# Top-k selection in a streaming encoder step: two jobs' rounds interleaved, the samples' rounds moved ahead of the delta stage

## The reference, cut to what matters

```python
score = einsum('bqh,bqhk->bqk', iw, relu(dots))           # index scores of every key
score = where(arange(L) < limit, score, -inf)
_, idx = lax.top_k(score, n_top)                            # n_top = min(256, L // 4)
logits = einsum('bqgrd,bqkgd->bqgrk', q, k_all[idx]) * A_HEAD_DIM ** -0.5
p = softmax(where(valid, logits + bias, -inf))
...                                                         # gated delta rule, chunks of 64:
sol = triangular_solve(eye + m, concat([v * beta, kb * exp(gc)]))
```

## Time and profile before

| | us |
|---|---|
| median of 3 runs | 1452.32 (1452.25 to 1454.1) |
| the profiled execution | 1452.18 |
| its span | 1450.3 |
| PE busy | 1395.6 |
| DVE busy | 901.2 |
| ACT busy | 565.4 |
| POOL busy | 387.7 |

### The profile page before, as it was taken

How to read it: one execution, slowest core, us unless ns; L and a number is a source line. 1 busy time by engine, 2 the same in 40 slices (tenths; PEclk the granted TensorE clock), 3 DMA queues, 4 the chain that set the end, 5 groups by cost and what they waited for, 6 DMA issues and landing times. The chain is left out here.

```text
span 1450.3 us, 28858 instructions
## 1 busy us (share of the span) xinstructions
PE 1395.6 (96%) x11611; PEld 1309.1 (90%) x11611; DVE 901.2 (62%) x1661; ACT 565.4 (39%) x1125; POOL 387.7 (27%) x352
## 2 busy tenths in 40 slices
PE   5999999999999999999999899898999999999997
PEld 4999999999999989999896667798999999999997
DVE  5546775575477452577778886745567458744864
ACT  5422431332243352654335435535443134413444
POOL 1603322330242241432011221024541235203500
PEclk9999999999999999999999999999999999999999
DMA  9634444455443324222205031241224123331231
GB/s 333 184 124 138 143 159 136 146 168 168 131 144 104 105 57 98 74 68 59 59 23 148 6 90 60 67 131 44 59 59 131 44 59 88 110 95 50 73 97 73
DMA packets 207657, 148.77 MB, mean 103 GB/s; under 512 B 21163, under 2 KB 191436, under 8 KB 207528
## 3 DMA queue, kind: packets, MB, share of 16 engines
q1 hardware_dynamic: 204360, 137.54, 31.7%
q0 software_dynamic: 3168, 9.42, 2.4%
HBM read 139.99 MB, written 6.95 MB: 101 GB/s over the span
## 5 line engine op out<-in xcount | busy, mean ns | idle before, releaser
L1163 PE MATMUL pair<-b_hi,w_hi 128*128 128x320 f32 x720 | 224.3, 311 | 0.0
L1163 PE MATMUL pair<-b_hi,w_lo 128*128 128x320 f32 x720 | 222.5, 309 | 0.0
L1163 PE MATMUL pair<-b_lo,w_hi 128*128 128x320 f32 x720 | 222.4, 309 | 0.0
L1276 PE MATMUL pair<-act_hi,w_hi 128*128 128x320 f32 x656 | 150.8, 311 | 0.0
L1276 PE MATMUL pair<-act_lo,w_hi 128*128 128x320 f32 x656 | 149.5, 309 | 0.0
L1276 PE MATMUL pair<-act_hi,w_lo 128*128 128x320 f32 x656 | 149.4, 309 | 0.0
L548 DVE SCALAR_TENSOR_TENSOR x_t<-pair,gate,x_t 128x320 f32<-128x320 f32 x120 | 52.5, 480 | 153.8 <-PE pair L1276 128.9
L1163 PEld LDWEIGHTS pair<-b_hi,w_hi 128*128 128x128 f32 x720 | 135.1, 188 | 7.0 <-issue 4.5
L660 ACT ACTIVATE w_hi<-sums_a 128x512 fp32r<-128x512 f32 x72 | 45.2, 628 | 246.5 <-POOL sums_a L694 129.3
L1044 DVE TENSOR_TENSOR uvw<-pair,uvw 128x320 f32<-128x320 f32 (+1 forms) x126 | 67.6, 536 | 115.6 <-PE pair L1163 115.5
L1163 PEld LDWEIGHTS pair<-b_lo,w_hi 128*128 128x128 f32 x720 | 135.2, 188 | 0.0
(11 more groups left out here) (481 smaller groups left out, 3214.6 us busy)
## 6 DMA issues: line engine op xcount, KB each, us to landing
w_mod_raw<-w_mod SPq DMA_DIRECT2D x28, 1024.0 KB, 6.5
w_raw<-ffn_w_gate SPq DMA_DIRECT2D x40, 512.0 KB, 3.9
raw_more<-ffn_w_up SPq DMA_DIRECT2D x40, 512.0 KB, 3.8
w_raw<-w_in SPq DMA_DIRECT2D x22, 512.0 KB, 3.8
w_raw<-ffn_w_down SPq DMA_DIRECT2D x16, 384.0 KB, 3.6
raw_more<-ffn_w_down SPq DMA_DIRECT2D x16, 384.0 KB, 3.4
w_mod_a<-w_mod SPq DMA_DIRECT2D x4, 1024.0 KB, 11.1
w_mod_b<-w_mod SPq DMA_DIRECT2D x4, 1024.0 KB, 11.4
```

Source lines behind the costliest of these rows:

```text
L1163: mm = pe.matmul(job_bank(j, BANK_OF[part]), w[:, at, kk], mv[:, kk, s], start=(kk == 0 and v == 0 and part in FIRST_OF_BANK), stop=(kk == ...
L1276: mm = pe.matmul(pair[part % 2][:, b, 0:HALF], w[:, slot, k], mv[:, k, b * HALF:(b + 1) * HALF], start=(k == 0 and v == 0), stop=(k == n - ...
```

## The change

Four things are moved or rewritten; the number of MAX8 and MATCH_REPLACE8 stays the same.

1. Jobs 1 and 2 are done together by `topk_two`: `max` of job 1, `max` of job 2, `match_replace` of job 1, `match_replace` of job 2, with the eight values of each in its own half of `mx` (now 16 wide). It is written out, not a loop. `TWO_ROUNDS` gives the pairs of rounds per unit: 1, 1, 4, 4, 4 in `aq0` to `ak0`, and 2 in `gz0`, where both masks are made.
2. The samples' scores are copied in `gz1` with four of their rounds; the other four and the samples' mask are in `gz2`. In the delta stage nothing of them is left.
3. POOL waits for the first job's probabilities (`prob` at 2) ahead of the four `scale_v`.
4. So the fourth mask for which SP waits is made in `gz0`, no longer in the unit `gz2`.

```diff
-            ("mx", [P, 8], F32), ...
+            ("mx", [P, 16], F32), ...
...
             pool.dma_start(a["_k_s"][0].rearrange("b t g d -> (b t) (g d)"), k_tok[:, NT - 1]).then_inc(S["out_kv"], 16)
+            pool.wait_ge(S["prob"], 2)
             for t in range(NT - 1):
                 scale_v(t)
...
+            def topk_two(n, before):
+
+                s0, s1 = score_of(1), score_of(2)
+                for i in range(n):
+                    at = before + 2 * i
+                    if i:
+                        dve.wait_ge(S["mr"], at - 1)
+                    dve.max(mx[:, 0:8], s0).then_inc(S["mx"], 1)
+                    dve.wait_ge(S["mr"], at)
+                    dve.max(mx[:, 8:16], s1).then_inc(S["mx"], 1)
+                    dve.wait_ge(S["mx"], 2 * at + 1)
+                    dve.match_replace(s0, mx[:, 0:8], s0, NEG_TAKEN).then_inc(S["mr"], 1)
+                    dve.wait_ge(S["mx"], 2 * at + 2)
+                    dve.sem_inc(S["mx"], 2)
+                    dve.match_replace(s1, mx[:, 8:16], s1, NEG_TAKEN).then_inc(S["mr"], 1)
+                dve.wait_ge(S["mr"], before + 2 * n)
...
+            TWO_ROUNDS = {V["aq", 0]: 1, V["aq", 1]: 1, V["aq", 2]: 4, V["aq", 3]: 4, V["ak", 0]: 4, V["gz", 0]: ROUNDS - 14}
+            def choose_ahead(v):
+                n = v - SCORE_V - IDX_HEADS // PER_STEP
+                if 0 <= n < ROUNDS // 2:
+                    topk(0, 2, 2 * n)
+                    if n == ROUNDS // 2 - 1:
+                        make_mask(0)
+                if v in TWO_ROUNDS:
+                    done = sum(TWO_ROUNDS[u] for u in TWO_ROUNDS if u < v)
+                    topk_two(TWO_ROUNDS[v], ROUNDS + 2 * done)
+                if v == V["gz", 0]:
+                    make_mask(1)
+                    make_mask(2)
+                if v == V["gz", 1]:
+                    sample_scores()
+                    topk(3, TOPK_S // 8 // 2, 3 * ROUNDS)
+                if v == V["gz", 2]:
+                    topk(3, TOPK_S // 8 - TOPK_S // 8 // 2, 3 * ROUNDS + TOPK_S // 8 // 2)
+                    sample_mask()
...
-                if v >= SCORE_V + IDX_HEADS // PER_STEP and any(left[0:3]):
-                    next_rounds(2 if v <= V["g", 11] else 1 if v <= V["aq", 1] else 6)
-            while any(left[0:3]):
-                next_rounds(4)
-            sample_scores()
+                choose_ahead(v)
...
                 biased(j)
-                sample_rounds(1)
                 normed(j)
                 level_added(0, lv)
                 keys_in(lv + 1)
                 matrices(lv + 1)
                 if lv == 2:
                     level_begun(1)
-                if lv == 0:
-                    sample_rounds(1)
-            sample_rounds(1)
-            level(1, 0, lambda: sample_rounds(1), lambda: w_out(0))
-            level(1, 1, lambda: sample_rounds(1), place_own)
-            level(1, 2, both((sample_mask,), (new_v, 0)))
+            level(1, 0, None, lambda: w_out(0))
+            level(1, 1, None, place_own)
+            level(1, 2, lambda: new_v(0))
```

More of the change, by code:

```diff
@@ L1326, in encoder_step @@
             ("q_var", [P, NT, GH], F32), ("o_ss", [P, NT, GH], F32), ("o_std", [P, NT, GH], F32), ("o_r", [P, NT, GH], F32),
[L1327 removed]
+            ("mx", [P, 16], F32), ("l_min", [P, 2], F32), ("l_sum", [P, 2], F32), ("l_inv", [P, 2], F32),
             ("iw_s", [P, NT, 8], F32), ("zz", [P, NT, GH], F32), ("z_abs", [P, NT, GH], F32),
@@ L2051, in topk @@
                 with dve.Fori(0, n) as i:
-                    dve.max(mx[:], s).then_inc(S["mx"], 1)
+                    dve.max(mx[:, 0:8], s).then_inc(S["mx"], 1)
                     dve.wait_ge(S["mx"], 2 * before + 1 + 2 * i)
                     dve.sem_inc(S["mx"], 1)
-                    dve.match_replace(s, mx[:], s, NEG_TAKEN).then_inc(S["mr"], 1)
+                    dve.match_replace(s, mx[:, 0:8], s, NEG_TAKEN).then_inc(S["mr"], 1)
                     dve.wait_ge(S["mr"], before + 1 + i)
+            def topk_two(n, before):
[13 more added lines that the diff above has]
+                dve.wait_ge(S["mr"], before + 2 * n)
             def make_mask(job):
@@ L2089, in sample_mask @@
             def sample_mask():
-                link(dve.max(mx[:], score_s))
-                link(dve.memset(mx[:, TOPK_S % 8:], NEG_TAKEN))
-                link(dve.match_replace(score_s, mx[:], score_s, NEG_TAKEN))
+                link(dve.max(mx[:, 0:8], score_s))
+                link(dve.memset(mx[:, TOPK_S % 8:8], NEG_TAKEN))
+                link(dve.match_replace(score_s, mx[:, 0:8], score_s, NEG_TAKEN))
                 make_mask(3)
@@ L2226, in mix_dve @@
             dve.wait_ge(S["cols"], 1)
-            delta_dve(dve, link, next_rounds, sample_mask, *attention_dve(dve, link))
+            delta_dve(dve, link, *attention_dve(dve, link))
             dve.wait_ge(S["st_out"], 16)
@@ L2234, in mix_dve, with delta_dve @@
                 add_to_x(dve, 1, U_OUT + m, m, X_OUT + m, U_OUT + m + 2)
-        def delta_dve(dve, link, sample_rounds, sample_mask, biased, normed, place_own):
+        def delta_dve(dve, link, biased, normed, place_own):
             def matrices(q):
```

## The result

| | median of the runs shown, us | lowest to highest | profiled execution | its span |
|---|---|---|---|---|
| before | 1452.63 (4 runs) | 1452.25 to 1454.10 | 1452.18 | 1450.3 |
| changed | 1444.81 (4 runs) | 1444.57 to 1445.15 | 1444.67 | 1442.8 |

The ratio is 0.9945, 95% interval 0.9933 to 0.9957: the change makes the kernel faster, by 7.8 us or 0.55%. The forecast was 1447.5 with a range from 1444.9.

A forecast was written before the change was run, and what follows sets the result against it. PE, busy 96% of the span, was taken as the bound; gains only from its waits and slow clock. 0.15 + 0.85 + 1.65 + 0.75 + 1.3 = 4.7 us off 1452.2 gave 1447.5, range 1444.9 to 1450.3.

The forecast's parts named there:

- first job's wait, what is left at the second: First attention job: PE's 1.32 us wait for scaled probabilities goes whole, but only 0.15 is left at the second job.
- levels of the second and third job: Delta stage, second and third job: DVE gets ahead but PE, being full, doesn't; gain 0.
- fourth job: At 792.76: decays come 1.0 us earlier with `biased`; 0.85 of PE's 1.04 us wait is gained.
- fifth job: At 801.00: without the samples' rounds ahead of and behind `biased`, 1.65 of PE's 1.88 us wait is gained.
- sixth job with the clock: At 808.88: 0.75 of the 1.09 us wait gained, plus 1.3 from the half-speed stretch at 801.7 going.
- if it waits for all four (...), it ends at 772.1: First job: DVE's `m_mat`, held until POOL's four scalings end, ends at 772.1 instead of 770.94 us.
- Rival 1: POOL lets DVE in between two scalings: `m_mat` held a few tenths, 1.0 us more gain, 1446.5; chance 0.15.
- In levels 1 and 2 PE is full: Second and third job's levels: PE busy throughout, so removing the samples' rounds there gains 0.
- The clock's part: From 801.7 to 805.0 PE runs at half clock behind the 1.88 us wait; the stretch should go, gaining 1.3 us.
- rival 4: End of projections: the pair hides no waits (3.7 us each), PE waits for ACT's root, 1460; chance 0.05.
- Rival 3: Sample jobs behind: loads of cached keys pace them, so the gain is given back later, 1451.5; chance 0.1.
- Rival 2: Delta stage: the clock falls all the same, 1448.8, or 1450.5 with a second slow stretch; chance 0.2.

The follow-up runs named there:

- e2: The changed kernel without POOL's wait for the first job's probabilities; 1445.99 us, ratio 0.9966 to the kernel before.
- e8: The changed kernel with POOL's wait at 1 instead of 2, for the first scaling of probabilities only; 1445.31 us, ratio 0.9955.
- e10: The changed kernel with 24 spare POOL multiplications ahead of the scalings, each waiting for the one just before; 1448.76 us, one run.
- e9: The changed kernel with 24 spare POOL multiplications in SBUF ahead of the scalings, each waiting for the one three before; 1453.67 us, one run.
- e5: The changed kernel with POOL's wait at 10 instead of 2, behind the fifth job's probabilities; 1443.93 us, ratio 0.9943.
- e6: The changed kernel with a spare round of the samples' size in the second and the third level; 1444.99 us, ratio 0.9953.
- e11: The changed kernel with spare rounds in four places of the fourth, fifth and sixth job; 1447.85 us, ratio 0.9970.
- e3: The changed kernel with the samples' rounds and mask back in the delta stage, pairs and POOL's wait kept; 1452.28 us, ratio 0.9999.
- e4: The changed kernel with the rounds of jobs 1 and 2 not interleaved, each in its own loop; 1458.31 us, ratio 1.0050.
- e1: The kernel before with only POOL's wait for the first job's probabilities added; 1452.19 us against 1452.09, ratio 1.0007.
- e12: The changed kernel with the last of POOL's four scalings of `s_in` waiting for the eighth job's probabilities; 1444.99 us, ratio 0.9946.
- e7: The changed kernel with two spare rounds, ahead of and in the fifth job; 1444.62 us, ratio 0.9949.

## Why the prediction was wrong in size

The mechanism stands in the main: the pairs make room, the samples' rounds leave a line of work that PE waits for, POOL and DVE no longer meet at the first job, and the slow stretch at 801 is gone. Term by term, with the increments of the table of jobs:

| step | forecast | measured |
|---|---|---|
| first job's wait, what is left at the second | 0.15 | 2.10 |
| levels of the second and third job | 0 | 0.21 (2.31 - 2.10) |
| fourth job | 0.85 | 1.01 |
| fifth job | 1.65 | 2.08 |
| sixth job with the clock | 0.75 + 1.3 | 2.21 |
| sum in the stage | 4.7 | 7.61 |
| start of the stage; front of FFN2 | 0; 0 | +0.84; -1.63 |

Of the 2.9 us that the sum lacks, 1.35 lie in the first step (the 1.50 of the first job is kept, where 0.15 was forecast), 0.81 in levels that were taken as full (0.60 and 0.21) and 0.75 in the fourth to the sixth job.

**The step that failed** is "if it waits for all four (...), it ends at 772.1", and with it the 0.15 that was left of 1.32. `m_mat` wasn't held to the end of POOL's run: it took 0.43 us in all, and `qk_m` behind it 1.15. Rival 1 (POOL gives way between two scalings) is what happened. The forecast had taken one row, the probabilities that let an end of POOL's go by at 767.65, for a rule; e2 shows that hold again and e8 the other behaviour with the same instruction. The Trainium skill ("SBUF — State Buffer", section "Who interferes with whom") says that whoever issues first has the shared pair (of SBUF ports, which DVE and GpSimd share) for its whole instruction. The changed kernel and e10 agree with it (one POOL instruction at most); the 1.85 us of the earlier trace rows, the 2.72 of e2 and the 3.33 of e9 don't, since one or two ends went by. Had I gone by the Trainium skill here, the forecast would have been rival 1's 1446.5, in the range and nearer. The loss from the meeting is nil (e5). By the estimate under e8 a hold over the whole run would have left 0.6 us at the second job, not far from the 0.15: what followed from the premise was sized nearly rightly, and it is the premise, the hold itself, that was wrong. What decides it stays open.

**"In levels 1 and 2 PE is full"** was wrong as well, by less than it sounds. The busy share of 7.60 of 7.60 hides waits of a tenth of a microsecond under overlapping records, and PE was in fact following DVE: with DVE ahead the level takes 7.39 (e6). That is the 0.21 of the third job (7.60 to 7.39), and in the same way the 0.60 that the second job gained beyond the 1.50 of the first (7.99 to 7.39).

**Fourth to sixth job**: each right in kind, each too small, by 0.16, 0.43 and 0.16. For the fifth the sum left 0.2 of the 1.88 us of waiting; there is none, and the interval to it fell by 2.08, more than the wait, for the same reason as above (the fourth job's transposes take 1.04 us instead of 1.25). The clock's part, 1.3, was well met: 1.36 by e11, a single profile. That the stretch follows from the wait of 1.88 us was the reason given for it, and e11 shows that wait without the stretch. The stretch comes and goes with the samples' rounds (e3), but not through that wait alone, so this part was right for a reason that isn't shown.

**Points that held**: nothing from the earlier transposition, from SP's earlier loads and from the later splits (e3); transposition at 749 (748.89); POOL from 767.7 (from 766.66, of which 0.84 is the earlier start of the stage); price of rival 4, with some luck (e4). The pair took 2.24, just below the 2.3 to 2.7, and so DVE was ready for the transposition 10 us earlier than before and not 5; the time of the transposition was right because it is PE's squares that set it. Rival 3, given back later, didn't occur: between the seventh job and the output projection nothing is lost. Rival 2 occurred in one sense: not at 801, but the stretch in front of FFN2 was 3.41 us longer and cost 1.63 in the profiled execution. That this and the 0.84 us ahead of the stage nearly cancel in the profiled difference is chance.

**Left open**: what makes the clock fall at 801 with the samples' rounds in the stage and not with the same waits without them (e11), and what decides whether a run of POOL instructions without waits lets DVE in at its next end or at a later one.

## What to carry to other kernels

A chain of short instructions that each wait for the one before (here rounds of MAX8 and MATCH_REPLACE8, 3.7 us for two) gets its waits filled by a second, independent chain (2.24), but that pays only through what is moved into the room: look for the work that stands between two instructions that the bound engine waits for, and take it to where that engine is full. A window with PE busy for 100% doesn't prove that PE sets the pace; compare the length of the same level, or of the same group of matmuls (1.25 and 1.04 us here), where its feeder is ahead. The level was 0.2 to 0.6 us less. Before a delay on another engine is charged to the bound one, look for its slack (0.73 us of holding cost nothing here, e5), and before one row's hold is taken for a rule, look for a second.

## What the runs showed of the hardware

- A DVE instruction with SBUF inputs that meets a POOL one is most often let in at the end of the POOL instruction that runs, and ends 0.28 us later, or 0.55 for a two-input one of 128x512 (e9, e10). POOL's own instruction, 1.04 us alone, is then 1.22 long in e9 and 1.10 in e10; the four scalings are 4.39 instead of 4.03.
- In POOL's runs of four without a wait between them a DVE instruction let one end go by (1.85 us, before) or two (2.72, e2; 3.33, e9), having come 0.47, 0.60 and 0.28 us into one of them. In runs of the same kind others were let in at the first end (e8 at 0.11 and 0.13 us into one, the changed kernel at 0.35, e10 at 0.23 to 0.35). Neither the kind of the instruction nor how far the POOL one had got tells these apart by itself. The runs that held one over an end all began directly behind POOL's DMA issues, and those that began behind the wait for probabilities (changed, e1, e4, e8, e12) held none over; but e10's four began behind DMA issues too and held none over. Where each POOL instruction waited for the one before, none was held beyond the first end.
- The stretches at half clock that ended within the profile had lengths of 3.41, 6.83 or 10.24 us. That in front of FFN2 is in every profile, at either of the two longer lengths with the same work ahead of it. The way from the output projection to FFN2 took 65.6 to 66.1 us with the shorter one (before, e2, e7, e8) and 66.6 to 67.8 with the longer. The difference, 0.5 to 2.2 us, is of the size of the largest single term of the forecast (1.65).
